# First mixer of a two-block network: gated projections first, one convolution tile on ScalarE and GpSimd, token transform by even and odd tokens

## What is computed

```
p = h @ w_in                                  # 1024 -> 1536
pa, pu, pg = split(p, [512, 1024])
ya = real(fft2(pa as (L, 4 groups, 128), over tokens L and over the 128 channels, ortho))
u  = pu * sigmoid(pg)
u  = depthwise_conv(u, conv_w, 31 taps, padding 15) + conv_b     # 512 channels
yb = silu(rmsnorm(u, conv_g))
return concat(ya, yb) @ w_out                 # 1024 -> 1024
```

## Time and profile before

| | us |
|---|---|
| median of 3 runs | 3448.82 (3448.72 to 3452.2) |
| the profiled execution, its own time | 3450.24 |
| its span | 3448.4 |
| PE busy over the span | 3056.5 (89%) |
| DVE busy | 1190.9 (35%) |
| ACT busy | 746.5 (22%) |
| POOL busy | 511.5 (15%) |

### The profile page before, as it was taken

How to read it: one execution, slowest core, us unless ns; L and a number is a source line. 1 busy time by engine, 2 the same in 40 slices (tenths; PEclk the granted TensorE clock), 3 DMA queues, 4 the chain that set the end, 5 groups by cost and what they waited for, 6 DMA issues and landing times.

```text
span 3448.4 us, 36261 instructions
## 1 busy us (share of the span) xinstructions
PE 3056.5 (89%) x15306; PEld 2108.4 (61%) x15306; DVE 1190.9 (35%) x2233; ACT 746.5 (22%) x1338; POOL 511.5 (15%) x487
## 2 busy tenths in 40 slices
PE   5988799989858899889999949999997888899987
PEld 3757555454446565474545537888556775588875
DVE  3983300000045332311000034322546773432234
ACT  3122211111132143201111123222112232222222
POOL 0210122222210043023232210000003221000000
PEclk8998799999979999889999979999996899999998
DMA  6510799999831231369999942223011002122220
GB/s 235 193 55 24 310 352 404 412 396 401 336 127 60 86 123 50 139 265 403 415 413 394 406 141 74 99 96 122 31 66 74 1 1 98 49 98 88 97 91 36
DMA packets 132024, 625.93 MB, mean 182 GB/s; under 512 B 14079, under 2 KB 85887, under 8 KB 97424
## 3 DMA queue, kind: packets, MB, share of 16 engines
q0 software_dynamic: 40160, 403.75, 29.0%
q1 hardware_dynamic: 90544, 214.80, 17.5%
q10 hardware_dynamic: 1152, 4.98, 0.4%
HBM read 617.18 MB, written 29.36 MB: 187 GB/s over the span
## 4 chain that ended last, share of the span: by engine, by line
PE 61%; DMA 15%; DVE 7%; ACT 2%; issue 2%; POOL 1%; SPq 0%; ACTq 0%; POOLq 0%; DVEq 0%
PE ps L92 59%; DMA ring<-in_exp_up,wix 13%; PE ps L95 2%; DVE scr L106 2%; DVE scr L126 1%; ACT hT L98 1%; DVE hT L114 1%; DVE scr L120 1%; DMA hrows<-scr 1%; DVE hT_r L106 1%; DVE xT L114 0%; DVE scr L114 0%; POOL ring L135 0%; DVE ring_r L106 0%; ACT scr L98 0%
## 5 line engine op out<-in xcount | busy, mean ns | idle before, releaser
L92 PE MATMUL ps<-ring,scr 128*64 128x512 f32 (+3 forms) x3136 | 744.5, 568 | 65.6 <-DMA ring<-in_exp_up,wix 64.2
L92 PE MATMUL ps<-ring_r 128*128 128x512 f32 (+1 forms) x2544 | 754.7, 379 | 37.2 <-DVE hT_r L106 36.6
L92 PEld LDWEIGHTS ps<-ring_r 128*128 128x128 f32 x2544 | 472.0, 192 | 151.0 <-issue 47.9
L92 PEld LDWEIGHTS ps<-ring,scr 128*64 128x64 f32 (+2 forms) x3136 | 300.9, 158 | 423.0 <-issue 412.7
L92 PE MATMUL ps<-scr,ring 128*128 128x128 f32 (+2 forms) x3744 | 489.1, 295 | 41.3 <-DMA ring<-yrows 21.7
L92 PEld LDWEIGHTS ps<-scr,ring 128*128 128x128 f32 x3744 | 457.9, 202 | 70.1 <-issue 51.9
L92 PE MATMUL ps<-hT_r,ring_r 128*128 128x512 f32 (+1 forms) x1224 | 462.6, 378 | 0.0
L106 DVE TENSOR_TENSOR scr<-scr,ps 64x512 f32<-64x512 f32 (+1 forms) x72 | 49.7, 690 | 775.2 <-ACT scr L98 446.5
L92 PEld LDWEIGHTS ps<-hT_r,ring_r 128*128 128x128 f32 x1224 | 235.8, 193 | 40.5 <-issue 2.0
L92 PE MATMUL ps<-scr_r,ring_r 128*128 128x512 f32 x1104 | 259.6, 396 | 0.6 <-DVE scr_r L106 0.6
L102 ACT ACTIVATE scr<-ps 128x512 f32<-128x512 f32 (+3 forms) x227 | 118.9, 535 | 579.6 <-PE ps L92 411.6
(11 more groups left out here) (136 smaller groups left out, 2539.6 us busy)
## 6 DMA issues: line engine op xcount, KB each, us to landing
ring<-in_ffn_w SPq DMA_DIRECT2D x66, 1024.0 KB, 5.3
ring<-in_mod_w SPq DMA_DIRECT2D x12, 2048.0 KB, 7.5
ring<-in_mod_w SPq DMA_DIRECT2D x16, 1024.0 KB, 4.8
scr<-in_mod_w SPq DMA_DIRECT2D x8, 1024.0 KB, 8.4
ring<-in_exp_gate SPq DMA_DIRECT2D x4, 2048.0 KB, 14.8
ring<-in_exp_up SPq DMA_DIRECT2D x4, 2048.0 KB, 17.5
ring<-in_exp_down SPq DMA_DIRECT2D x4, 2048.0 KB, 22.1
ring<-in_w_in SPq DMA_DIRECT2D x4, 2048.0 KB, 8.1
```

The source lines that it names most:

```text
L92: return self.real.matmul(o, l, r, start=start, stop=stop) if self.real else Quiet()
```

## The change

- Jobs go gated 0, 1, 2, 3, plain 0, plain 1, on TensorE and in the loads.
- The convolution of tile 2 leaves DVE. ACT multiplies the shifted input by each tap's weight into one of two buffers (`taps`, 31 activations, two or three after each product from job 3 on), and POOL adds each to `AC` (30 `tensor_tensor`).
- DVE runs `conv(0)`, `conv(1)`, `conv(3)`, cut in other places around the `gated(m)` steps.
- The token transform takes even and odd tokens apart. Each half is a matmul of half the width, the even and odd sums share a bank, ACT copies the even half to H (`even`), and DVE makes sum and difference (`odd`).
- The norm's matmuls are placed among those of the token transform: the sum after groups 0 and 1 of the 512 chunk, the root after groups 2 and 3, then the 256 chunk.
- The low parts of `H(0..3)` are made by POOL, those of job 6 by DVE.

```
-POOL_LOWER = [("f", j) for j in range(2, 8)] + [("at", 0), ("at", 1), ("ffn1_", 1, 0), ("ffn1_", 3, 0)]
+POOL_LOWER = [("f", j) for j in (2, 3, 4, 5, 7)] + [("at", 0), ("at", 1), ("ffn1_", 1, 0), ("ffn1_", 3, 0)]
...
     def pe_fourier(e):
...
-        gated(0, 0)
-        plain(0, 1)
-        gated(1, 2)
-        plain(1, 3)
-        gated(2, 4)
-        gated(3, 5)
+        for m in range(4):
+            gated(m, m)
+        for q in range(2):
+            plain(q, 4 + q)
...
+                        t = r + 256 * i
+                        e.matmul(o[:, 0:256], PA(g, a, n)[:, t:t + 255:2], k("dft"), True, True).then_inc(
+                            *ps.fill("f_t", a, r, i, g))
...
+        over_tokens(0, 512, 0)
+        over_tokens(0, 512, 1)
+        pe_norm_sum(e, st_conv)
+        over_tokens(0, 512, 2)
+        over_tokens(0, 512, 3)
+        wr.done(("f_dft", 0), "f_y", 0, 3)
+        pe_norm_root(e, st_conv)
+        for g in range(4):
+            over_tokens(512, 256, g)
...
     def act_fourier(e):
...
+        def taps(n):
+
+            for j in range(tapped[0], min(tapped[0] + n, 31)):
+                w = vec("conv_w", 2 * 31 + j)
+                if j == 0:
+                    e.wait_ge(*ps.emptied("f_up", 2, 0))
+                    e.wait_ge(*ps.emptied("f_up", 2, 512))
+                    i = e.activation(F.ac[:, 2 * 783:3 * 783], UP(2, 0, 783), ACT.Identity, bias=vec("conv_b", 2), scale=w)
+                else:
+                    if j > 2:
+                        e.wait_ge(*pool_step.of("conv", 2, j - 2))
+                    i = e.activation(F.tap[j % 2], UP(2, j, 783), ACT.Copy, scale=w)
+                i.then_inc(*act_step.up("tap", j))
+                tapped[0] = j + 1
...
+            if j >= 3:
+                taps(2 + g % 2)
...
+        taps(31)
+        for o in st_conv.order[0:4]:
+            e.wait_ge(*dve_step.of("conv", 1, 30))
+            act_square(e, st_conv, *o)
...
+        e.wait_ge(*pool_step.of("conv", 2, 30))
+        for o in st_conv.order[4:6]:
+            act_square(e, st_conv, *o)
         e.wait_ge(*dve_step.of("conv", 3, 30))
-        for o in st_conv.order:
+        for o in st_conv.order[6:8]:
             act_square(e, st_conv, *o)
...
     def dve_fourier(e):
...
-        for m in range(2):
-            gated(m)
-            conv(m)
+        gated(0)
+        conv(0, 0, 18)
+        gated(1)
+        conv(0, 18)
+        conv(1, 0, 4)
         gated(2)
-        conv(2, 0, 18)
+        conv(1, 4, 21)
         gated(3)
-        conv(2, 18)
+        conv(1, 21)
         conv(3)
         for o in st_conv.order:
             dve_sum(e, st_conv, *o)
+        part_lower(e, ("f", 6))
+
+        def odd(a, n, g):
+            h, o = n // 2, ps.ap("f_y", a, g)[:, n // 2:n]
+            e.wait_ge(*act_step.of("f_even", a, g))
+            e.tt(H(g, a + h, h), H(g, a, h), o, SUB)
+            e.tt(H(g, a, h), H(g, a, h), o, ADD).then_inc(*ps.empty("f_y", a, g))
+        odd(0, 512, 0)
+        odd(0, 512, 1)
         dve_norm(e, st_conv)
+        odd(0, 512, 2)
+        odd(0, 512, 3)
+        for g in range(4):
+            odd(512, 256, g)
...
     def pool_fourier(e):
         e.memset(F.up, 0.0).then_inc(*pool_step.up("f_pad"))
-        for j in range(2, 8):
+        for j in range(2, 5):
             part_lower(e, ("f", j))
+
+        o = F.ac[:, 2 * 783:3 * 783]
+        e.wait_ge(*act_step.of("tap", 0))
+        for j in range(1, 31):
+            if j == 11:
+                part_lower(e, ("f", 5))
+            e.wait_ge(*act_step.of("tap", j))
+            if j > 1:
+                e.wait_ge(*pool_step.of("conv", 2, j - 1))
+            e.tt(o, o, F.tap[j % 2], ADD).then_inc(*pool_step.up("conv", 2, j))
+        part_lower(e, ("f", 7))
+        for kt in range(4):
+            hi, lo = f_mix(kt)
+            e.wait_ge(*h_hi.of("f_mix", kt))
+            e.tt(lo, H(kt), hi.bitcast(F32), SUB).then_inc(*h_lo_pool.up("f_mix", kt))
```

More of the change, by code:

```diff
@@ L645, in pe_product8 @@
         for kt in range(8):
-            e.wait_ge(*h_lo.of(lo_of, kt))
+            e.wait_ge(*(h_lo_pool if lo_of == "f_mix" and kt < 4 else h_lo).of(lo_of, kt))
             m = mm3(e, o[:, 0:n], parts(key, step * kt + c), x(kt, a, n), kt == 0, kt == 7)
@@ L709, in pe_fourier @@
-        pe_norm(e, st_conv)
+        for m in range(4):
+            gated(m, m)
+        for q in range(2):
+            plain(q, 4 + q)
+        for a, n in chunks(768):
+            for r in range(2):
+                for i in range(n // 256):
+                    for g in range(4):
+                        o = ps.take("f_t", a, r, i, g)
+                        e.wait_ge(*ps.ready("f_t", a, r, i, g))
+                        e.wait_ge(*ps.emptied("f_pa", g, a))
+                        t = r + 256 * i
+                        e.matmul(o[:, 0:256], PA(g, a, n)[:, t:t + 255:2], k("dft"), True, True).then_inc(
+                            *ps.fill("f_t", a, r, i, g))
@@ new lines, in over_tokens @@
+        def over_tokens(a, n, g):
+            h, ni = n // 2, n // 256
+            e.wait_ge(*wr.there("f_dft", a))
+            o = ps.take("f_y", a, g)
+            e.wait_ge(*ps.ready("f_y", a, g))
+            e.wait_ge(*ps.emptied("f_t", a, 1, ni - 1, 3))
+            for r in range(2):
+                for i in range(ni):
+                    x = F.tb[a][:, ((r * ni + i) * 4 + g) * 256:((r * ni + i) * 4 + g) * 256 + 256]
+                    e.matmul(o[:, h * r:h * r + h], x[:, 0:128], weights(("f_dft", a), h, r * ni + i, 0, h), i == 0, False)
+                    m = e.matmul(o[:, h * r:h * r + h], x[:, 128:256], weights(("f_dft", a), h, (2 + r) * ni + i, 0, h), False,
+                                 i == ni - 1)
+            m.then_inc(*ps.fill("f_y", a, g))
@@ L710, in pe_fourier @@
+        over_tokens(0, 512, 0)
[7 more added lines that the diff above has]
+            over_tokens(512, 256, g)
+        wr.done(("f_dft", 512), "f_y", 512, 3)
         for m in range(8):
@@ L730, in mods @@
                     mod_columns(e, mod0b, columns.pop(0))
-            for u, half in after_group(m, g):
+            for u, half in after_group(j, g):
                 if half:
@@ L777, in act_fourier @@
                 e.activation(H(4 + c, a, n), AC(c, a, n), ACT.Silu).then_inc(*act_step.up("f_silu", c, a))
-        for kt in range(8):
-            e.wait_ge(*(ps.emptied("f_y", 512, kt) if kt < 4 else act_step.of("f_silu", kt - 4, 512)))
-            e.copy(f_mix(kt)[0], H(kt)).then_inc(*h_hi.up("f_mix", kt))
+            if c:
+                e.wait_ge(*act_step.of("f_silu", c - 1, 512))
+                e.copy(f_mix(3 + c)[0], H(3 + c)).then_inc(*h_hi.up("f_mix", 3 + c))
+        e.wait_ge(*act_step.of("f_silu", 3, 512))
+        e.copy(f_mix(7)[0], H(7)).then_inc(*h_hi.up("f_mix", 7))
         part_upper(e, ("f", 8))
@@ L829, in dve_fourier @@
                     *dve_step.up("conv_n", c, a))
-        for kt in range(8):
+        for kt in range(4, 8):
             hi, lo = f_mix(kt)
```

93 lines of the change are left out of this document (47 added, 46 removed).

## The result

| | before | after |
|---|---|---|
| median, us | 3448.50 (3440.82 to 3452.2, 16 runs) | 3455.65 (3445.88 to 3463.91, 16 runs) |
| ratio | | 1.0024 (1.0015 to 1.0034) |
| the profiled execution, its own time | 3450.24 | 3445.88 |
| its span | 3448.4 | 3444.1 |

The change makes the kernel 7.15 us slower. The forecast was 3455.0. The profiled execution of the kernel after is a short one: TensorE waited 55.4 us in it for the experts' weights and 64.2 in the kernel before, in stages that the change leaves alone. So times are compared by medians, and in the traces I compare marks inside the mixer. Three of them serve for every kernel here. S is the start of DVE's convolution (the first tap of tile 0, or DVE's first step after `gated(0)` where a low part stands there), T the end of DVE's last tap, M the start of the second output product.

What follows compares the result with a forecast made beforehand. DVE's convolution, ending with the token transform near 249, then a chain to the second output product were taken as the bound. 246 + 36.5 = 282.5, 5.3 later: 3450.24 becomes 3455.5, medians 3454, said 3455; range 3440 to 3468.

Steps and rivals of the forecast that it cites:

- T: End of DVE's convolution: 204.0 without adds plus 42 for 30 adds, 246 (238 to 254), where it was 249.
- Turns between POOL and DVE: In the convolution, POOL's two-input work shuts out DVE's taps: adds 2.4 to 2.5 us apart, 1.4 lost each.
- bounds 1.13 and 1.65: DVE's loss per POOL add: 1.13 us if each instruction hides a fixed 0.47, 1.65 if nothing hides.
- TensorE's pause: TensorE stands still about 16 us near 160, waiting for DVE's fourth gated step to empty a bank; counted as nothing.
- ACT's queue: ACT copies `f_t` only after its taps, from about 230 to 241; two `f_y` groups then end at 248.
- the 19 that are left end at 184 + 46.5 = 231: POOL's remaining 19 adds, resumed at 184 and taking 2.45 us each in turns with DVE, end at 231.
- The third rival: ACT's queue arrives last: adds of 2.0 us, TensorE ends at 256, time near 3467; chance 0.19 (including a costlier add).
- The tail: Convolution's end to second output product: sums, root, `f_y`, scaling beside POOL's low parts, 36.5 us, where it was 28.2.
- From the mark to the time: Second output product's start moves 5.3 us later, to 282.5, and the end with it; medians to 3454, said 3455.
- The first rival: POOL does not hold DVE up in the convolution: it ends at 204, second output product 238, time near 3412; chance 0.12.

Runs made afterwards that it cites:

- the tile given back: Changed kernel with tile 2 of the convolution back on DVE, without ACT's taps and POOL's adds: 3451.25 us, ratio 1.0013.
- the early `gated`: Changed kernel with the fourth gated step on DVE behind 6 taps instead of 17: 3460.13 us, ratio 1.0035.
- the narrow adds: Changed kernel with POOL's 30 adds cut from 783 to 64 columns, same instructions and waits: 3418.43 us, ratio 0.9916.
- after once more: The changed kernel, unaltered, measured again in the third series: 3455.12 us, ratio 1.0023.
- `f_y` first: Changed kernel with all eight groups of the token transform ahead of the norm's column sums: 3444.59 us, ratio 0.9991.
- low parts on DVE: Changed kernel with the low parts of H(0..3) on DVE behind the scaling, instead of on POOL beside it: 3450.91 us, ratio 1.0006.

## Why the prediction was right

**Turns between POOL and DVE.** Right. Adds were to start 2.4 to 2.5 us apart; they start 2.39 apart, and taps beside them take as long. An add was priced at 1.4 us of DVE, bounds 1.13 and 1.65; the runs show 1.34, by the lengths and by the tile given back. Its own length was put at 1.6, and the shortest takes 1.57. Of the two bounds the lower one had the right form, a fixed part hidden in each add, and its 0.47 us is 0.2 to 0.3. By the rule of the Trainium skill ("SBUF — State Buffer", section "SBUF: two separate sides"), the pair locked for the full instruction, 30 adds were estimated at 48 us. The runs show 40, so DVE is shut out for most of an add but not all of it. One thing the prediction read too narrowly: it names taps with two inputs, but the first tap of a tile, which has one input tensor, is held up too (2.25 us beside adds in the kernel after, 0.69 alone).

**T.** Forecast 246, and 246.51 in the trace. That it is so close is in part luck. The prediction counted four low parts on POOL beside the taps, and there are five, so that DVE is spared one of them and not two. Counted from S, three tiles without adds take 118.8 us where it has 115.9, and the adds 40.2 where it has 42. The two misses have opposite signs.

**TensorE's pause.** Forecast 16 us near 160, ended by `gated`; 14.12 from 159 to 173. The prediction counted nothing for it, and the early `gated` shows that it is off the path.

**ACT's queue.** Off by 6 us. Copies of `f_t` were to begin at about 230 and start at 224.4. The step that failed is "the 19 that are left end at 184 + 46.5 = 231". It was 19, but they resume at 181.07 and take 2.39 each, so that they end at 226.6, and ACT, a tap or two ahead, is free 2 us before that. So the two sides did not meet at 248 as laid out. TensorE was through with groups 0 and 1 at 241.1 and waited 9.36 us for DVE's sums. The third rival, in which this side is last, was farther away than its 0.19 said, and its own numbers do not put it there: with an add of 2.0 us it has TensorE through at 256 and T at 258, and its 3467 follows from T. Its bound of 2.6 us for a turn held T still, but a dearer add moves T by 30 adds and this side by 19 turns only. The side ends last where adds are cheap, as with 64 columns.

**The tail.** Forecast T + 36.5, and T + 38.2 in the trace. By steps: column sums at T + 4.0 (3.9 forecast), root at T + 15.3 (13.7), the last `odd` of DVE ends at T + 21.9 (20.4), scaling at T + 32.4 (30, where its own terms add up to 30.5), the last low part at T + 36.1 (34), M at T + 38.2. The mis-sized term is `f_y` of groups 2 and 3. It was priced at 7.1 us by a row with no long pause just ahead of it, and takes 8.94. (The two windows below have length, busy time and count of PE, PEld, DVE, ACT and POOL, the granted clock, the DMA share and GB/s.) The first two groups take 7.07 at a granted clock of 1.00:

```profile
234.10:241.10 7.00, 7.00 (x33) 5.85 (x31) 6.79 (x7) 0.50 (x2) 0.00 (x0) 1.00 0.00 0
...
253.10:261.90 8.80, 8.80 (x34) 7.46 (x34) 1.91 (x9) 0.59 (x2) 0.00 (x0) 0.80 0.00 0
```

Groups 2 and 3 stand behind the wait of 9.36 us, at a mean clock of 0.80. Where there is no such wait in front of them, with the narrow adds, they take 7.15. The scaling beside POOL's low parts was forecast at 10.1 and takes 10.58; without them it is 4.33.

**From the mark to the time.** M moved by 7.4 us in the two traces and by 8.0 counted from S, against 5.3 forecast. The medians moved by 7.15. The forecast of 3455.0 is nearer to 3455.65 than its steps were: it was made from a median of 3448.82 and rounded up from 3454. What the steps missed is 2 to 3 us, 1.7 of it in the tail. So the mechanism is right and the last 2 us of agreement are luck.

**The first rival** asked what the change would be worth if POOL did not hold DVE up: near 3412. With adds of 64 columns, which cost DVE nothing, it is 3418. T came as the rival has it (204.5, against 204), M at 245.5 and not at 238: TensorE was through with groups 0 and 1 at 215.0 instead of 211, and POOL's low parts of H still stand beside the scaling, which takes 10.59 us.

## What to carry to other kernels

Before work is moved from VectorE to GpSimd, look in the trace of the kernel for a row where the two already run beside each other, and charge VectorE for GpSimd's time. Here 33 us taken off VectorE cost it 40 us of waiting, and a low part that GpSimd made "for free" cost VectorE up to 4.2 us where VectorE itself does it in 2.3. In a chain of short steps that hangs on a late result, put the work that does not depend on it ahead of the chain, in the wait, and not between its steps. And halving work that is hidden can pay only together with what shortens the engine that hides it; this last is argued from two traces and has no run of its own.

## What the runs showed that I had not expected

- The shortest adds cost DVE nothing at all: with 64 columns the three tiles take 118.9 us, with no adds 118.8, though beside the taps an add then takes 0.90 us in the median, and 0.30 at the shortest. The price starts somewhere between 64 and 392 columns.
- S to T is 159.0 us in four traces (after, after once more, `f_y` first, low parts on DVE), so this mark repeats far better than whole times (3435 to 3467 us over those kernels' runs). T to M repeats less well, 38.2 and 39.2 us in the two traces of the kernel after. With marks a few us of a stage can be read from one trace.
- In the norm chain a pause of TensorE made the 32 matmuls behind it slower: 7.15 us without one (narrow adds), 8.58 to 9.71 us behind pauses of 9.4 to 32.2 us, at a granted clock of 0.73 to 0.83. The longest pause does not cost the most (9.20 us behind 32.23, 9.71 behind 21.29, 9.58 behind 10.95); why they differ is open. A wait that looks harmless on an idle engine has this tail where the chain goes on over the same engine.
